# A transformer trunk on one core: the first modulation chunk under the output products is loaded between the third and the fourth block of output weights

## What is computed

```
for layer in range(DEPTH):                                   # DEPTH = 2
    sh1c, sc1c, g1c, sh2c, sc2c, g2c = modulation(c_ctx[None], w_mod[layer], b_mod[layer])
    sh1l, sc1l, g1l, sh2l, sc2l, g2l = modulation(c, w_mod[layer], b_mod[layer])
    hc = rms_norm(xc, norm1[layer]) * (1 + sc1c) + sh1c      # hl likewise
    ...                                                      # attention and a second mixer, side by side
    out = jnp.concatenate([...], axis=-1) @ w_out            # the output products, (640 x 1024) @ (1024 x 1024)
    xc = xc + g1c * oc                                       # xl likewise
    hc = rms_norm(xc, norm2[layer]) * (1 + sc2c) + sh2c
    xc = xc + g2c * ec_moe(hc, ...)                          # 16 experts, each with its own three matrices

def modulation(cvec, w_mod, b_mod):
    m = jax.nn.silu(cvec) @ w_mod + b_mod                    # w_mod: 1024 x 6144 for each layer
    return [p[:, None, :] for p in jnp.split(m, 6, axis=-1)]
```

## Time and profile before

| | us |
|---|---|
| median of 3 runs | 1390.81 |
| lowest and highest | 1388.46, 1392.39 |
| profiled execution, its own time | 1387.17 |
| span of the profile, first to last instruction | 1385.0 |

### The profile page before, as it was taken

How to read it: one execution, slowest core, us unless ns; L and a number is a source line. 1 busy time by engine, 2 the same in 40 slices (tenths; PEclk the granted TensorE clock), 3 DMA queues, 4 the chain that set the end, 5 groups by cost and what they waited for, 6 DMA issues and landing times.

```text
span 1385.0 us, 18165 instructions
## 1 busy us (share of the span) xinstructions
PE 1263.4 (91%) x7550; PEld 911.6 (66%) x7550; DVE 870.2 (63%) x1013; ACT 705.5 (51%) x819; POOL 235.9 (17%) x133
## 2 busy tenths in 40 slices
PE   5999988899399999999789998999984999999997
PEld 2897856788266666666469984667872666666662
DVE  5613546423678888888385252553344899999994
ACT  3531146611467777777343124554123777776772
POOL 3100000011302222211030000000124033333330
PEclk9997899999699999999899999899996999999996
DMA  9710182042799999999883222002419999999974
GB/s 364 247 63 31 33 277 104 1 153 92 275 369 357 384 379 380 385 391 397 290 276 103 95 68 72 1 1 92 153 41 381 379 376 377 385 383 382 393 294 161
DMA packets 100472, 324.98 MB, mean 235 GB/s; under 512 B 6720, under 2 KB 30495, under 8 KB 84007
## 3 DMA queue, kind: packets, MB, share of 16 engines
q1 hardware_dynamic: 89376, 290.88, 55.7%
q0 software_dynamic: 8400, 27.58, 7.7%
q10 hardware_dynamic: 2614, 5.35, 1.0%
HBM read 300.29 MB, written 23.50 MB: 234 GB/s over the span
## 4 chain that ended last, share of the span: by engine, by line
PE 74%; DMA 8%; ACT 7%; DVE 6%; POOL 2%; issue 1%; SPq 0%; ACTq 0%; POOLq 0%; DVEq 0%
PE psum L944 71%; ACT arena L1814 4%; DVE arena L2270 2%; DMA stage<-in_moe_w_up 2%; DVE w_lo L2000 2%; DMA h_hi<-h_dram,arena 1%; POOL arena L891 1%; PE psum L1464 1%; DMA stage<-in_moe_w_gate 1%; DMA h_dram<-arena 1%; DMA stage<-in_w_mod 1%; DMA arena<-in_x_sample 1%; DMA arena<-in_od_w_in 1%; ACT arena L1581 1%; ACT w_hi L1890 1%
## 5 line engine op out<-in xcount | busy, mean ns | idle before, releaser
L944 PE MATMUL psum<-w_hi,h_hi 128*80 128x512 f32 (+1 forms) x848 | 330.4, 390 | 8.4 <-DVE w_lo L2000 5.0
L2000 DVE TENSOR_TENSOR w_lo<-stage,w_hi 128x2048 fp32r<-128x2048 f32 (+1 forms) x122 | 275.5, 2270 | 99.5 <-ACT w_hi L1594 59.5
L944 PE MATMUL psum<-w_lo,h_hi 128*80 128x512 f32 (+1 forms) x848 | 326.0, 384 | 0.0
L944 PE MATMUL psum<-w_hi,h_lo 128*80 128x512 f32 (+1 forms) x848 | 325.7, 384 | 0.0
L1890 ACT ACTIVATE w_hi<-stage 128x2048 fp32r<-128x2048 f32 x100 | 190.6, 1915 | 60.2 <-PE psum L944 37.0
L944 PE MATMUL psum<-h_hi,w_hi 128*128 128x320 f32 x672 | 212.4, 316 | 2.0 <-DVE h_lo L2047 2.0
L944 PE MATMUL psum<-h_lo,w_hi 128*128 128x320 f32 x672 | 209.7, 312 | 0.0
L944 PE MATMUL psum<-h_hi,w_lo 128*128 128x320 f32 x672 | 209.6, 312 | 0.0
L909 POOL DMA_INDIRECT acc_dram<-arena x31 | 120.2, 3878 | 413.0 <-ACT arena L1922 227.8
L2000 DVE TENSOR_TENSOR w_lo<-arena,w_hi 128x2048 fp32r<-128x2048 f32 x73 | 166.7, 2288 | 31.0 <-ACT w_hi L1890 28.2
L944 PEld LDWEIGHTS psum<-w_hi,h_hi 128*80 128x80 f32 (+1 forms) x848 | 129.9, 153 | 82.5 <-issue 13.7
(11 more groups left out here) (275 smaller groups left out, 1289.8 us busy)
## 6 DMA issues: line engine op xcount, KB each, us to landing
stage<-in_w_mod SPq DMA_DIRECT2D x46, 1024.0 KB, 9.0
stage<-in_moe_w_up SPq DMA_DIRECT2D x36, 1024.0 KB, 15.7
stage<-in_moe_w_down SPq DMA_DIRECT2D x34, 1024.0 KB, 15.0
stage<-in_moe_w_gate SPq DMA_DIRECT2D x30, 1024.0 KB, 15.2
arena<-in_moe_w_gate SPq DMA_DIRECT2D x29, 1024.0 KB, 16.2
arena<-in_moe_w_up SPq DMA_DIRECT2D x23, 1024.0 KB, 15.4
arena<-in_moe_w_down SPq DMA_DIRECT2D x19, 1024.0 KB, 15.5
xT<-in_moe_w_down SPq DMA_DIRECT2D x11, 1024.0 KB, 19.5
```

Of the source, the lines that this page charges most:

```text
L944: return pe.matmul(o, w, x, start=first, stop=last, skip_group_check=True)
L2000: return nc.vector.tensor_tensor(dst, src, hi.bitcast(F32), ALU.subtract)
```

## The change

The list of loads gets another order in both layers. The first of the chunks under the output products (8 in layer 0, 20 in layer 1) moves ahead of the last block of output weights. The remaining chunks keep their order behind that block. No piece is added or removed, and what PE, ACT, DVE and POOL do, and in which order, stays as it is; since slots are given in turn, three pieces of each layer move to another slot and wait for another piece to be done.

```
-            out(0), out(1), mod("qk"), mod("first scores"), out(2), out(3)
+            out(0), out(1), mod("qk"), mod("first scores"), out(2)
         else:
             out(0), out(1), mod("cq")
             for n in range(2):
                 stream.append(dict(key=(L, "lent", n), split=False, used=(L, "O", PAIRS), p=len(stream), q=None, src=None, place=staged()))
-            out(2), out(3)
-        mod((L, "out")), mod((L, "rank"))
+            out(2)
+        chunk(MOD_AT[(L, "out")][0])
+        out(3)
+        for c in (*MOD_AT[(L, "out")][1:], *MOD_AT[(L, "rank")]):
+            chunk(c)
```

## The result

| | before | changed |
|---|---|---|
| median | 1389.43 us (6 runs) | 1381.68 us (6 runs) |
| lowest and highest | 1388.46, 1392.39 | 1375.86, 1385.18 |
| profiled execution, its own time | 1387.17 | 1379.99 |
| span of the profile | 1385.0 | 1377.8 |

The ratio is 0.9928, with an interval of 0.9906 to 0.9950. By that ratio it is 10.0 us less, between 6.9 and 13.1. The two medians of the table are only 7.8 us apart (their quotient is 0.9944): with six runs on each side, two ways of summing up the same runs differ by 2 us. The forecast was 6.0 less.

What follows compares the result with a forecast made beforehand. PE, holding 91% of the span, was taken as the bound; removing two waits on late loads under the output products, 3.08 + 2.94 = 6.0 us, from 1390.8 gave 1384.8 us, range 1381.0 to 1388.8.

Steps and rivals of the forecast that it cites:

- 9b and 21b: Second halves of chunks 9 (layer 0) and 21 (layer 1): loads go out earlier, both PE waits vanish whole, slack at least 5.7 us.
- The sum of 6.0 us: Gain from both PE waits under the output products: 3.08 us in layer 0 plus 2.94 us in layer 1.
- The new tenants: Loads 10b, 22b and out(3) in their new slots or order: still in time, cost nothing; out(3) in layer 1 has 6.6 us cover.
- Downstream: Behind the output products, ranking, gathering and experts move forward with PE, so the 6.0 us survive to the end.
- Clock gives part back: Rival, chance 0.15: PE reaches the experts earlier but the clock rise doesn't; net gain 1.5 to 4.2 us, about 1388 us.
- neither wait moved: Rival, chance 0.06: the stall at chunk 9 hides another, so at most one layer gains; 1387.8 us.
- both are gone: Rival, chance 0.03: 9b still doesn't go out before 294.2 because another piece ahead on SP waited; nothing changes, 1390.8 us.
- new stretch of 24 us at half clock: Slower rival, chance 0.04: moved timing makes one more such stretch under full PE work, costing 12 us; 1396.8 us.
- The stretch with the stall itself has clock 1.00: At the stalls under the output products, no clock is won or lost by the change.
- The lateness of 20b: Layer 1's second half of chunk 20 moves from second to first load after attention: no loss, perhaps a tenth gained.
- about 2 us either way for a median of few runs: Scatter allowed in the forecast case's own range, 1382.5 to 1386.6 us, from three runs spread over 3.9.
- mostly while PE idles: Three page slices at clock 0.6 each hold about 24 us at half clock, said to fall mostly in PE's idle time.

Runs made afterwards that it cites:

- the fillings: Changed kernel plus extra unread matmuls while PE waits before the experts; ratios to the kernel before 0.9932, then with more of them 0.9896 and, repeated, 0.9931.
- K's count: Over profiles of kernels with the short PE pause, the clock fell behind one of eight, costing 2.8 us; estimated 0.7 us for the two pauses together.

## Why the prediction came out as it did

**9b and 21b.** Right. The forecast had 9b issued "about 1 us" behind the start of chunk 8; it went out at 281.57, 1.12 us behind 280.45, and 21b at 964.89, 1.13 us behind 963.76. The waits went as a whole, as forecast.

**The sum of 6.0 us.** Right in the trace to 0.05 us: 3.08 and 2.94 were forecast, and 3.09 and 2.96 measured over the stretches. It was right to take 6.0 and not the recorded idle time of 5.6.

**The new tenants.** Right. Chunk 10 stands as one run at 313.59, though 10b now waits for the split. ACT took `out(3)` in layer 1 at 974.79, earlier than the 976.54 of the earlier trace rows by what PE had shifted, and no wait is recorded there:

```profile
974.79 1.90 ACT L1597 ACTIVATE w_hi<-stage 128x2048 fp32r<-128x2048 f32 x1
```

**Downstream.** Right. The rankings are 39.9 and 42.2 us as before, and PE's first products of the experts follow by the same distance. That everything moves forward with PE holds for a gain ahead of the experts; the 2 us that the fillings gained at the first expert of layer 1 did not last to the tail. "Clock gives part back" did not come about: the first experts took 10.18 to 11.22 us in layer 0 and 10.04 to 10.44 in layer 1 in four profiles of the changed kernel, against 10.79, 11.00 and 10.48, 10.21 in two of the kernel before. The other rivals are out by the same rows: neither wait moved, both are gone, and no new stretch of 24 us at half clock appeared.

**The step that failed** is the sentence "The stretch with the stall itself has clock 1.00, so no clock is won or lost at the place of the change." One execution showed 1.00 there. Another shows 0.50 behind the same pause, at a cost of 2.8 us, and where the pause was 5.2 us long it fell both times. So the sum lacked a term: the chance that a pause costs clock, times what that costs. By the count above it is 0.7 us, and in a single execution it can be 2.8 or 5.6. The forecast used the clock only as a danger to its gain, and not as part of what the pause already cost. The lateness of 20b in one of five profiles is a second term of the same sign, some 0.2 us on average. The missing terms are small: with 6.95 in the place of 6.0 the forecast would have been 1383.9, still 3.1 us above the 1380.8 of the ratio, and a range moved along with it would just have held the result.

**The size of the first measurement** is not explained by that. The changed kernel was timed four times: by the ratios 10.0, 6.7, 6.0 and 8.5 us less, each with some 2.3 to 3.1 either way. Weighted by their intervals they make a ratio of 0.9947, 7.4 us less, between 6.1 and 8.8. So 6.75, and 6.95 with the term for 20b, lie inside, 6.0 just below it, and 10.0 is high by no cause that any run shows: the scatter of six runs is enough for it. That is the second step that failed, the width. The forecast took "about 2 us either way for a median of few runs" from three runs that spread over 3.9 us. 33 runs of the kernel before on one chip went from 1382.31 to 1397.84, and the spread of three was a poor measure of that. A range for this kernel needed some 3 us on each side for scatter alone.

The clocks of the single runs split the gain. The 93 runs of the kernel before and the 38 of the changed kernel that have a clock on record average 1390.1 and 1382.3 us, 7.8 us apart (6.7 to 9.0), with 141.6 and 137.3 us at half clock, 4.3 us less (1.1 to 7.5). From run to run of one kernel, each us at half clock goes with 0.32 us of time. At equal time at half clock the changed kernel is 6.5 us faster (5.8 to 7.1), which holds the 6.05 of the traces, and the clock makes the other 1.4, of which K's count gives 0.7. An estimate, but it says that there is little left to explain: the wait, the clock that the wait cost, and a first measurement that came out high.

Where the scatter sits can be read. The sixteen matmuls of 64 rows in the tail, before and in the changed kernel:

```profile
1355.25 13.53 PE L944 MATMUL psum<-arena 64*128 64x512 f32 x16 [1.46 <-DVE arena L2445]
```

```profile
1350.39 7.54 PE L947 MATMUL psum<-arena 64*128 64x512 f32 x16 [1.47 <-DVE arena L2448]
```

The same work at two clocks, 6 us apart in PE's time, of which 2.3 show up in the tail. The change has no part in it: the second repeat of the changed kernel has the longest tail of all (32.6 us, with a granted clock of 0.57 from 1350 on), the third one of the two shortest (24.9).

## What to carry to other kernels

A load list that is walked in order and shares slots between pieces of different lifetimes makes a stall where a late piece's slot is held by something that is itself late: follow the slot's former tenant, not the bandwidth, and try first whether two neighbours in the list can swap. Price such a stall as first matmul to next product against an undisturbed neighbour, and then ask whether PE's clock falls behind it in some executions: one profile that shows 1.00 doesn't say so for the others, and the mean clocks of all timed runs do. When the expected gain is of the size of the scatter, take the scatter from many runs of one kernel and repeat the comparison before explaining the excess.

## What the runs showed of the hardware

**A short pause of PE has two prices.** Behind pauses of 2.7 to 3.0 us the granted clock stayed at 1.00 seven times and fell to 0.50 once; behind pauses of 5.2 to 5.3 us it fell both times. A fall cost 2.8 us in the one case and 2.3 and 1.6 us in the others.

**The clock falls under a busy PE as well.** In the kernel before, two stretches (columns as above):

```profile
120.00:150.00 30.00, 30.00 (x126) 17.45 (x126) 9.73 (x11) 2.21 (x3) 0.00 (x0) 0.57 0.00 1
1356.00:1366.00 10.00, 10.00 (x12) 3.18 (x11) 3.41 (x4) 2.59 (x6) 0.00 (x0) 0.52 0.71 262
```

PE is counted busy for the whole of both, with small matmuls (the second stretch holds the 64-row products), and the granted clock is 0.57 and 0.52. The forecast said of such stretches that they lie "mostly while PE idles". It is also why a busy share of 91% says little on how fast PE works. And it goes with the scatter: over the 93 runs of the kernel before, the time and the time at half clock are correlated at 0.83, and of the stretches in the table the tail moves most.

**Time at half clock is not time lost.** Filling the pauses before the experts took over 30 us of half clock out of the kernel, and the 2 us that it gained at the first expert of layer 1 came back as waits for weights (4.1 and 4.8 us against 1.8 to 2.8).
